# A two-layer decoder trunk on one core: last modulation block in eight places of its own, rounding ahead of the squares, sums of modulation between products

## The reference, cut to what matters

```python
def reference(x, c, ...):                # x (1, 256, 1024), c (1, 1024), float32; DEPTH = 2
    c_act = jax.nn.silu(c)
    for i in range(DEPTH):
        mod = c_act @ w_mod[i] + b_mod[i]                         # w_mod[i]: 1024 x 6144
        sh1, sc1, g1, sh2, sc2, g2 = jnp.split(mod, 6, axis=-1)
        h = modulate(rmsnorm(x, norm1_g[i]), sh1, sc1)            # h * (1 + scale) + shift
        if i == 0: y = short_conv_mixer(h, conv_w_in, conv_w, conv_w_out)   # 3 blocks in, 1 out
        else:      y = pool_mixer(h, pool_w_in, pool_w_grp, pool_scale, pool_w_out)
        x = x + g1[:, None, :] * y
        h = modulate(rmsnorm(x, norm2_g[i]), sh2, sc2)
        x = x + g2[:, None, :] * peer_ffn(h, peer_w_q[i], peer_k1[i], peer_k2[i],
                                          peer_u[i], peer_v[i])   # 16384 experts, all computed here
    return rmsnorm(x, final_g)
```

## Time and profile before

| | us |
|---|---|
| three timed runs | 2017.86, 2010.63, 2015.74 (median 2015.74) |
| profiled execution, its own time | 2009.94 |
| its span, first to last instruction | 2008.2 |
| PE busy | 1920.6 (96%) |
| DVE busy | 1537.9 (77%) |
| ACT busy | 855.6 (43%) |
| mean granted PE clock | 0.976 of full |
| read from HBM | 366.47 MB, 184 GB/s over the span |

### The profile page before, as it was taken

The page is one execution under the profiler, slowest core; times in us unless marked ns, Lnnn a source line. Parts: engine busy times, 40 slices in busy tenths (PEclk is TensorE's granted clock), DMA queues, the critical chain, the costliest instruction groups (busy, mean ns, idle before and its releaser), DMA issues.

```text
span 2008.2 us, 46305 instructions
## 1 busy us (share of the span) xinstructions
PE 1920.6 (96%) x17828; PEld 1905.8 (95%) x17828; DVE 1537.9 (77%) x2886; ACT 855.6 (43%) x1277; POOL 4.0 (0%) x8
## 2 busy tenths in 40 slices
PE   5987899999999999999999789999999999999998
PEld 5987899999999999999999789999999999999998
DVE  7974578997888888778868557988788888885554
ACT  3323344444334444444444434444443444434443
POOL 0000000000000000000000000000000000000000
PEclk9987999999999999999989899999999999999999
DMA  7963555554444544688844454555544454455552
GB/s 297 321 236 116 189 168 183 181 184 156 153 157 146 168 157 157 207 315 291 301 164 148 156 199 160 183 180 182 164 157 151 141 168 159 158 183 179 178 183 99
DMA packets 101342, 370.41 MB, mean 184 GB/s; under 512 B 11168, under 2 KB 11552, under 8 KB 100640
## 3 DMA queue, kind: packets, MB, share of 16 engines
q1 hardware_dynamic: 100848, 367.43, 54.4%
q10 hardware_dynamic: 432, 2.23, 0.3%
HBM read 366.47 MB, written 3.15 MB: 184 GB/s over the span
## 4 chain that ended last, share of the span: by engine, by line
PE 81%; DVE 8%; DMA 5%; issue 3%; ACT 2%; SPq 1%; ACTq 0%; DVEq 0%
PE ps L1058 37%; PE acc L1058 37%; PE gp L1151 5%; DVE acts L555 2%; DMA raw<-query 2%; DVE low L536 2%; ACT high L357 2%; PE gp L1018 1%; DMA raw<-conv_in 1%; PE gp L1140 1%; DVE acts L608 1%; DMA acts<-w_mod 1%; PE gp L1029 0%; DMA raw<-up 0%; DMA raw<-conv_out 0%
## 5 line engine op out<-in xcount | busy, mean ns | idle before, releaser
L536 DVE TENSOR_TENSOR low<-raw,high 128x1024 fp32r<-128x1024 f32 x596 | 727.0, 1221 | 410.2 <-ACT high L357 404.1
L357 ACT ACTIVATE high<-raw 128x1024 fp32r<-128x1024 f32 x593 | 626.0, 1056 | 579.0 <-PE acc L1058 427.4
L1058 PE MATMUL ps<-mov_h,high 128*128 128x256 f32 x2704 | 788.6, 292 | 40.9 <-ACT acts L459 21.5
L1058 PE MATMUL ps<-mov_l,high 128*128 128x256 f32 x2704 | 775.9, 287 | 0.0
L1058 PE MATMUL ps<-mov_h,low 128*128 128x256 f32 x2704 | 775.3, 287 | 0.0
L1058 PE MATMUL acc<-mov_h,high 128*128 128x256 f32 x2048 | 586.6, 286 | 1.4 <-DVE mov_l L958 1.4
L1058 PE MATMUL acc<-mov_l,high 128*128 128x256 f32 x2048 | 580.5, 283 | 0.0
L1058 PE MATMUL acc<-mov_h,low 128*128 128x256 f32 x2048 | 580.4, 283 | 0.0
L1058 PEld LDWEIGHTS ps<-mov_h,high 128*128 128x128 f32 x2704 | 528.7, 196 | 47.8 <-ACT acts L459 23.5
L1058 PEld LDWEIGHTS ps<-mov_l,high 128*128 128x128 f32 x2704 | 529.8, 196 | 0.0
L1058 PEld LDWEIGHTS ps<-mov_h,low 128*128 128x128 f32 x2704 | 529.3, 196 | 0.0
(11 more groups left out here) (101 smaller groups left out, 735.3 us busy)
## 6 DMA issues: line engine op xcount, KB each, us to landing
raw<-up SPq DMA_DIRECT2D x256, 512.0 KB, 3.3
raw<-down SPq DMA_DIRECT2D x256, 512.0 KB, 3.3
acts<-w_mod SPq DMA_DIRECT2D x84, 512.0 KB, 4.5
raw<-query SPq DMA_DIRECT2D x32, 512.0 KB, 4.6
raw<-conv_in SPq DMA_DIRECT2D x24, 512.0 KB, 6.8
acts<-w_mod SPq DMA_DIRECT2D x6, 1024.0 KB, 16.0
raw<-conv_out SPq DMA_DIRECT2D x8, 512.0 KB, 6.8
raw<-pool_in SPq DMA_DIRECT2D x8, 512.0 KB, 3.3
```

What stands on the lines that cost most here:

```text
L357: nc.scalar.activation(flat(high[s]), tile_row(s), ACT.Copy).then_inc(high_ready, 1)
L536: nc.vector.tensor_tensor(flat(low[n % RING]), tile_row(n % RING), flat(high[n % RING]).bitcast(F32), ALU.subtract).then_inc(low_ready, 1)
L1058: ins = nc.tensor.matmul(dst, w[s][:, c], m[:, mv], start=(first and n == 0), stop=(last and n == 2), skip_group_check=skip)
```

## The change

Three edits, and what hangs on them.

1. Block 5 is loaded into the eight places `mhead[:, 1, k]`, one semaphore each (`gate2_in`), so that no load waits for an earlier tile of this block to be used up; it waits that block 3's tile has left the place (layer 0) or that Z is made (layer 1). The query loop of SP is written out. The places overlap `S`, so ACT waits once for `gate2_used` before it first writes S.
2. `round_and_square` rounds tile c + 3 before the square of chunk c - 1 (it was: rounding of c + 3, then the square of c).
3. In layer 0 the sum of block 2 moves from ahead of conv_out to behind its first tile, that of block 4 from behind conv_out to behind its fourth tile, and only block 3 is summed behind it. The taking of the sums on DVE moves with them.

```diff
 # SP, query stage
-                with sp.Fori(0, 16 // RING) as i:
-                    for s in range(RING):
-                        load(layer, "query", i * RING + s, s)
-                        if s % 2:
-                            sp.wait_ge(mtile_used, i * 2 + ((2 + layer) * DC + s // 2 + 1))
-                            w = w_mod[layer, :, 5 * D:6 * D].rearrange("(k p) n -> k p n", p=P)
-                            sp.dma_start(mtile[:, s // 2], w[bass.ds(i * 2 + s // 2, 1)].rearrange("a p n -> (a p) n")
-                                         ).then_inc(mtile_in[s // 2], 16)
+                for j in range(16):
+                    load(layer, "query", j, j % RING)
+                    if j % 2:
+                        k = j // 2
+                        if layer == 0:
+                            sp.wait_ge(shift2_used, k + 1)
+                        else:
+                            sp.wait_ge(z_ready, DC)
+                        sp.dma_start(mhead[:, 1, k], w_mod[layer, k * P:(k + 1) * P, 5 * D:6 * D]
+                                     ).then_inc(gate2_in[k], 16)
 # ACT, round_and_square
-                with act.Fori(0, DC // RING) as i:
-                    for s in range(RING):
-                        ahead(i, n0, s)
-                        act.wait_ge(evac_dve, i * RING + (2 + evac0 + s + 1))
-                        nc.scalar.activation(A[:, bass.ds(i * (RING * T) + (SQ0 + s * T), T)], ...
+                for c in range(DC + 1):
+                    if c < DC:
+                        ahead(c // RING, n0, c % RING)
+                    if c:
+                        act.wait_ge(evac_dve, 2 + evac0 + c)
+                        nc.scalar.activation(sq[:, c - 1], X[:, c - 1], ACT.Square).then_inc(sq_done, 1)
 # ACT, first scores
+                    if n == 0:
+                        act.wait_ge(gate2_used, DC * (layer + 1))
 # DVE, residual and around it
+                    if layer == 0 and c in (0, 4):
+                        finish_mod(0, (2,) if c == 0 else (4,))
                     dve.wait_ge(product, n0 + c + 1 + RING)
 ...
-                    finish_mod(0, (2,))
                     residual(AT[0, "conv_out"], 0)
-                    finish_mod(0, (3, 4))
+                    finish_mod(0, (3,))
 # DVE, query stage
-                        t = (2 + layer) * DC + k
-                        dve.wait_ge(mtile_in[k % 2], (t // 2 + 1) * 16)
-                        dve.wait_ge(mtile_used, 2 + t)
-                        add_mod(5, mtile[:, k % 2], k, k == 0).then_inc(mtile_used, 1)
+                        dve.wait_ge(gate2_in[k], (layer + 1) * 16)
+                        if k:
+                            dve.wait_ge(gate2_used, DC * layer + k)
+                        add_mod(5, mhead[:, 1, k], k, k == 0).then_inc(gate2_used, 1)
 # PE, layer 0
-                    pe.wait_ge(mtile_used, 2 + 2 * DC)
-                    sum_mod((2,))
-                    run(0, "conv_out", 8, evac_dve, 24)
+                    for j in range(DC):
+                        project(0, "conv_out", j // RING, j % RING, evac_dve, 24)
+                        if j == 0:
+                            pe.wait_ge(mtile_used, 2 + 2 * DC)
+                            sum_mod((2,))
+                        if j == 3:
+                            sum_mod((4,))
 ...
-                    sum_mod((3, 4))
+                    sum_mod((3,))
```

More of the change, by code:

```diff
@@ L198, in program @@
         next_used = sem("next_used")
+        gate2_in = [sem(f"gate2_in{n}") for n in range(DC)]
+        gate2_used = sem("gate2_used")
         macc_done = sem("macc_done")
@@ L239, in load @@
                 static = isinstance(j, int)
-                if not (static and n0 + j < RING):
+                if not static or n0 + j >= RING:
                     sp.wait_ge(low_ready, j + (n0 - RING + 1))
@@ L398, in norm @@
                 shift = mod[:, (3 * (k % 2)) * DC:(3 * (k % 2) + 1) * DC]
-                act.wait_ge(mod_taken, (2, 4, 6, 7)[k])
+                act.wait_ge(mod_taken, (2, 5, 7, 8)[k])
                 for c in range(DC):
@@ L422, in round_and_square @@
             def round_and_square(n0, evac0):
-                with act.Fori(0, DC // RING) as i:
-                    for s in range(RING):
-                        ahead(i, n0, s)
-                        act.wait_ge(evac_dve, i * RING + (2 + evac0 + s + 1))
-                        nc.scalar.activation(A[:, bass.ds(i * (RING * T) + (SQ0 + s * T), T)],
-                                             A[:, bass.ds(i * (RING * T) + s * T, T)], ACT.Square
-                                             ).then_inc(sq_done, 1)
+                for c in range(DC + 1):
[4 more added lines that the diff above has]
+                        nc.scalar.activation(sq[:, c - 1], X[:, c - 1], ACT.Square).then_inc(sq_done, 1)
             act.dma_start(keys, k_t[0]).then_inc(keys_in, 16)
@@ L1094, in _ @@
                     run(0, "conv_in", 24, evac_dve, 0)
-                    pe.wait_ge(mtile_used, 2 + 2 * DC)
-                    sum_mod((2,))
-                    run(0, "conv_out", 8, evac_dve, 24)
+                    for j in range(DC):
[5 more added lines that the diff above has]
+                            sum_mod((4,))
+                    moved[0] += 1
                     pe.wait_ge(shift2_used, DC)
-                    sum_mod((3, 4))
+                    sum_mod((3,))
                     square_sums(1)
@@ L1159, in _ @@
                     if n == 0:
-                        pe.wait_ge(mtile_used, 2 + (3 + layer) * DC)
+                        pe.wait_ge(gate2_used, DC * (layer + 1))
                         sum_mod((5,))
```

## The result

The changed kernel took 1956.91 us (median of 4 runs, 1951.68 to 1958.06), the kernel before beside it 2015.76 us (4 runs, 2010.63 to 2017.86): ratio 0.9711, 95% interval 0.9691 to 0.9732, a gain of 59 us where 51 were forecast. The span of the profiled execution is 1949.9 us against 2008.2.

The account below looks back on a forecast made before the run. PE, 96% busy, was held in the query stages by SP's waits for additions, conv_out by a ring of ACT and DVE. Terms 16.3 + 15.9 + 9.3 + 5.3 + 4.2 = 51.0 us off 2015.7 gave 1965 us, range 1957 to 1977.

Parts of the forecast that it names:

- Query stages, 16.3 and 15.9 us: Query stages of layers 0 and 1: without SP's waits for additions, PE at 2.87 us a tile; gains 16.3 and 15.9 us.
- Bounds: nothing above it, since PE cannot go faster.: Query stage, layer 0: gain at most 16.3 us, and 0 at the old pace of two tiles per 9.26 us.
- Rounding ahead, layer 0, 9.3 us: conv_out: of DVE's 11.1 us waits, 9.3 gained; given back: late rounding 0.9, block 4's taking 0.3, its sum 0.6.
- Sums, layer 0, 5.3 us: Behind conv_out: two sums taking 6.99 us become one of 1.7 at full clock; gain 5.3 us, lower end 3.5.
- Order of the first tile and the sum of block 2, 0 us: Start of conv_out: tile first, sum second, but DVE's first addition to X stays where it is; 0 us.
- Rounding ahead, layer 1, 4.2 us: pool_out: additions to X take 20.1 us instead of 24.35, with PE's 2.87 a tile as bound; gain 4.2 us.
- Loops written out, 0 us: Loops written out on SP, ACT and PE run as straight code at no cost; 0 us.
- Transfers near 270 GB/s: Query stages: a sign of being right, transfer load rising from 163 to 274 GB/s, bearable since conv_in ran 314.
- rival A: Query stages: transfers set the pace, 3.2 us a tile, price 10 us, time 1975; chance 0.11.
- The ring with 6.8 us of landing: Query stage: rounding, remainder and transfer for a `raw` place take 9.1 us, within the 11.5 of four PE tiles.
- C: Query loads stay tied to the additions through the place wait; only 18.8 us come, time 1997; chance 0.04.
- B: Mixers (conv_out, pool_out) do not yield, ACT's later squares or late roundings cost some 9 us, time 1974; chance 0.09.
- D: Query stages: clock stays low, 5.29 instead of 2.87 us a tile; slower, 2042 with all 32 tiles low; chance 0.02.

Follow-up runs that it names:

- all_again: The whole changed kernel run once more with no further edit, beside the kernel before: 1953.38 us, ratio 0.9693.
- tied: Changed kernel, but SP's load of w_mod tile k waits again for the addition of tile k - 2: 1990.79 us, ratio 0.9874 to before.
- only_ahead: Kernel before with only the rounding put ahead of the square: 2000.85 us, ratio 0.9925.
- only_sums: Kernel before with only the sums of blocks 2 and 4 moved between the tiles of conv_out: 2008.52 us, ratio 0.9963.
- only_places: Kernel before with only block 5 in eight places and SP's query loop written out: 1978.31 us, ratio 0.9810.
- later: Changed kernel with the last addition of block 4 moved behind the making of mov_l for conv_out: 1955.16 us, ratio 0.9702 to before.
- extra: Changed kernel with eight more 512 KB w_mod tiles loaded per query stage and never used: 1956.62 us, ratio 0.9706 to before.

## Why the prediction was right, and what it undersized

The direction and the mechanism held. The size came out 8 us larger than forecast, at the edge of the range, and in `all_again` beyond it; that the first median is still 1957 when rounded is luck. Point by point:

- *Query stages, 16.3 and 15.9 us.* Against the profile that the prediction used: 16.8 and 16.7. In layer 0, 10.9 us of this are idle time of PE and the other 5.9 its busy time (57.6 to 51.8 us for the same tiles), with the granted clock of the stage up from 0.88 to 0.95. `tied` shows that the wait of SP alone was the cause. The pace is as forecast: from the second tile's copying out to the last one's pass 40.3 us (157.66 to 197.97), 2.88 a tile. The first tile ran at low clock, with matmuls of 0.41 us.
- *"Bounds: nothing above it, since PE cannot go faster."* Here the sum was too small. The bound holds the time after, not the time before, and that was read from one profile on the short side. The four profiles with the old query loop (both of before, `only_ahead`, `only_sums`) have 68.5 to 72.3 and 67.9 to 73.0 us, 70.5 and 70.7 on average. Against these the changed kernel gains 38.2 us, not the 32.2 of the sum, and `only_places` gained 37.7 by the timed runs.
- *The carry-over to the median.* "I carry the gain over to the median" took the 5.8 us between profile and median as time that both kernels would spend. In number this did no harm: the changed kernel's profiled execution lay 5.2 us below its own median, so the spans differ by 58.3 us and the medians by 58.9. That both draws lay alike is chance. So 7.3 of the missing 7.9 us are already missing between the two profiles: 3.2 in conv, nearly all ahead of the first addition to X, 1.2 in the query stages, 0.5 in pool, and 2.4 in stretches that no edit touches (1.2 ahead of conv, 1.2 on the way to layer 1), which other profiles repeat only within 1.6 and 3.7 us.
- *Rounding ahead, layer 0, 9.3 us.* From the first to the last addition to X it took 32.83 us before (123.12 to 155.95) and 23.14 after: 9.7. The three things given back are there, in somewhat other sizes: one late rounding of 0.67 us behind the first tile (forecast 0.9), another of 0.60 behind block 4's sum (0.6), and 0.15 us for its taking with 0.39 of waiting for the product (0.3).
- *Sums, layer 0, 5.3 us.* 6.99 to 1.95: 5.0. The sum stood behind an idle time of PE of 1.2 us (forecast "about a microsecond") and ran near full clock, here and in `all_again` and `later`. In `tied` and `extra`, behind the same 1.2 us, it took 2.66 and 2.58 us with the clock granted at 0.69 and 0.72. So the full 5.3 us were a likely figure, not a sure one. Behind 5.5 us of idle time the same sum took 3.57 (`only_sums`, clock 0.50); behind 1.7 us two sums took 5.38 (`only_ahead`, 0.67). The Trainium skill's account (TensorE: Matmul & The Clock Gate, "HAM oscillation") is that idle gaps bring the low clock back. These rows agree with it in the order of the gaps, and show that at 1.2 us it happened in two profiles of five.
- *Order of the first tile and the sum of block 2, 0 us.* The prediction let the first addition to X stay where it was. From conv's first matmul to that addition pass 84.4 to 85.4 us in the six profiles without edit 3 and 81.7 to 84.4 in the six with it (`later` left out): 1.6 us less on average, 2.9 less between the two profiles of the prediction's pair. With the sum first it took 3.56 to 3.58 us at a granted clock of 0.50 or 0.51, in all six, and the tile behind it 4.5 to 5.4. With the tile first the sum took 1.84 to 2.01 us, at 0.91 to 1.00, in all six (full length of the rows, tails included), and the tile 4.4 to 5.5. The tile's matmuls bring the clock up, and the sum profits.
- *Rounding ahead, layer 1, 4.2 us.* 4.20 between the additions, PE's 2.88 us a tile as the new bound.
- *Loops written out, 0 us.* Wrong of SP's loop as it stood: written out alone it is worth about 5 us. It is no further term here, since the change removes the waits that it shortened.
- *Transfers near 270 GB/s.* They are 295 GB/s while query and w_mod tiles are loaded together [stretch above], and 218 over 46 us. The first seven query tiles and three w_mod tiles were loaded before the stage began, so the rest needs only 24 us of it. The size of the load mattered for rival A alone, and `extra` shows that there was room.
- *The ring with 6.8 us of landing.* 1.06 + 1.15 + 6.8 is 9.0, not 9.1; nothing hangs on it.

Of the rivals, A is refuted by the waits of PE and by `extra`, C by the waits of SP and by `tied`, B by the rows of both mixers and by `only_ahead`; for D the granted clock in the 46 us shown is 0.95.

Open: what moves the time ahead of the first addition to X by up to 2.5 us between profiles of kernels that are alike up to there, and whether the timed gain of `only_sums` (7.5) beyond the 4.0 in its conv stage is chance.

## What to carry to other kernels

Where one queue issues transfers for two consumers in program order, look at the wait of the transfer that nobody is in need of: it holds up the ones behind it, and a place of its own for each removes the whole chain. An engine that prepares work ahead should have that work before, not behind, an instruction that waits for the present result. And if a stage is bound by a chain of short waits, one profile is one draw: read the stage from several profiles before you put a bound on its gain.

## What was not expected of the hardware

- Register instructions between transfers of a loop on SP cost 0.38 us (0.76 against 0.38) a pair, 0.67 at the loop's turn, on a chain that runs through SP.
- A stage with five waits of up to 5 us scatters: 68.5 and 71.4, 67.9 and 73.0 us in two profiles of one program, with the clock granted low for about 96 and 109 us of the span. Without the waits the same stage repeats within 0.1 us in two profiles of one program, and within 1.0 us in five kernels.
- Eight more tiles of 512 KB a stage raised the time to landing from 3.6 to 6.3 us and the rate from 295 to 360 GB/s over 24 us, and cost PE nothing.
- Sixteen narrow matmuls took 3.57 us behind an idle stretch (clock 0.50) and 1.84 us behind a tile of wide ones (clock 1.00).
